# A hybrid layer's prompt block: a third slot for split weights, a new order on VectorE and ScalarE, and taps carried over

## What is computed

```python
h = rmsnorm(x) * (1 + sc1) + sh1
proj = h @ w_in                       # 1024 x 2592
q, k, v, r, zf, zb, ga, gg = split(proj)
gf = log_sigmoid(zf @ w_decay_f + b_decay_f) / TAU        # gb alike
o = gla(q, k, v, gf) + flip(gla(flip(q), ..., flip(gb)))  # chunks of 64 tokens
o = rmsnorm(o) * silu(r)
u = ga * sigmoid(gg)                                      # the GLU product
u = silu(layernorm(depthwise_conv(u, width=31)))          # the taps
x = x + gt1 * (concat(o, u) @ w_out)
# second half: 16 experts, each takes the tokens that score highest for it
x = x + gt2 * expert_choice_moe(rmsnorm(x) * (1 + sc2) + sh2)
```

## Time and profile before

| | before |
|---|---|
| median of 3 runs | 2449.94 us (2448.81 to 2450.29) |
| profiled execution | 2448.1 us, span from first to last instruction 2446.4 us |
| TensorE busy | 2254.9 us, 92% of the span |
| VectorE busy | 1652.5 us, 68% |
| ScalarE busy | 1187.4 us, 49% |
| chain that ended last | 58% of the span on TensorE, 5% on VectorE, 2% on DMA, 2% on ScalarE |
| mean granted TensorE clock | 0.958 |
| median time to landing of the ten stores of split tiles | 13.2 us |
| TensorE busy from 60 to 180 us | 91.9 of 120 us |
| TensorE busy from 180 to 300 us | 119.8 of 120 us |
| VectorE busy from 60 to 180 us | 99.0 of 120 us |

### The profile page before, as it was taken

One profiled execution on the slowest core, in us unless ns is written; L12 is line 12 of the kernel. 1 busy time (PEld: TensorE's weight loads), 2 busy tenths in 40 slices (PEclk: granted clock), 3 DMA queues, 4 the chain that ended last, 5 costly groups with the idle time before them and its releaser, 6 DMA issues.

```text
span 2446.4 us, 43724 instructions
## 1 busy us (share of the span) xinstructions
PE 2254.9 (92%) x16667; PEld 2061.4 (84%) x16667; DVE 1652.5 (68%) x2871; ACT 1187.4 (49%) x1933; POOL 731.4 (30%) x666
## 2 busy tenths in 40 slices
PE   3879999999996999965999999999999999999994
PEld 3768878788885677742999999999999999999994
DVE  1797979799788766448566656666556665566575
ACT  3747364553524444421655554555545555455652
POOL 1000000000001311100254454544545445554352
PEclk8889999999997999986999999999999999999997
DMA  6976666757747566353466677666776667766785
GB/s 227 381 272 219 215 237 233 262 190 261 226 133 260 172 195 203 97 171 112 159 201 187 190 198 208 197 187 188 199 211 194 189 185 203 211 190 190 259 267 193
DMA packets 281300, 505.90 MB, mean 207 GB/s; under 512 B 25793, under 2 KB 224318, under 8 KB 265312
## 3 DMA queue, kind: packets, MB, share of 16 engines
q1 hardware_dynamic: 241872, 377.94, 46.9%
q0 software_dynamic: 39312, 126.38, 19.3%
HBM read 405.74 MB, written 98.53 MB: 206 GB/s over the span
## 4 chain that ended last, share of the span: by engine, by line
PE 58%; DVE 5%; DMA 2%; ACT 2%; issue 1%; POOL 1%; SPq 0%; DVEq 0%; ACTq 0%; POOLq 0%
PE bank L1580 18%; PE bank L1582 18%; PE bank L1581 18%; DVE work_exp L2738 1%; DMA out_dram<-work_exp 1%; PE bank L1833 1%; DVE work_proj L2445 1%; PE bank L1899 1%; PE bank L1843 1%; PE bank L1851 1%; DMA work_exp<-x_rows 1%; ACT hl_exp L1174 0%; DVE work_exp L2984 0%; ACT work_exp L1214 0%; DMA work_exp<-in_b_mod_dram 0%
## 5 line engine op out<-in xcount | busy, mean ns | idle before, releaser
L1580 PE MATMUL bank<-act_hl_exp,hl_exp 128*128 128x288 f32 x3072 | 911.1, 297 | 18.3 <-DVE hl_exp L2901 9.8
L1581 PE MATMUL bank<-act_hl_exp,hl_exp 128*128 128x288 f32 x3072 | 908.2, 296 | 0.0
L1582 PE MATMUL bank<-act_hl_exp,hl_exp 128*128 128x288 f32 x3072 | 906.6, 295 | 0.0
L1580 PEld LDWEIGHTS bank<-act_hl_exp,hl_exp 128*128 128x128 f32 x3072 | 578.4, 188 | 19.8 <-DVE hl_exp L2901 10.7
L1582 PEld LDWEIGHTS bank<-act_hl_exp,hl_exp 128*128 128x128 f32 x3072 | 580.3, 189 | 0.0
L1581 PEld LDWEIGHTS bank<-act_hl_exp,hl_exp 128*128 128x128 f32 x3072 | 579.2, 189 | 0.0
L2901 DVE TENSOR_TENSOR hl_exp<-work_exp,hl_exp 128x1024 fp32r<-128x1024 f32 x192 | 231.3, 1226 | 217.7 <-ACT hl_exp L1174 217.7
L2901 DVE TENSOR_TENSOR hl_exp<-raw_exp,hl_exp 128x1024 fp32r<-128x1024 f32 x192 | 232.1, 1224 | 202.5 <-ACT hl_exp L1174 202.5
L2445 DVE SCALAR_TENSOR_TENSOR work_proj<-work_proj,wcv 128x392 f32<-128x392 f32 (+11 forms) x600 | 337.3, 635 | 0.6
L1174 ACT ACTIVATE hl_exp<-work_exp 128x1024 fp32r<-128x1024 f32 x192 | 199.2, 1055 | 210.4 <-PE bank L1582 205.2
L1174 ACT ACTIVATE hl_exp<-raw_exp 128x1024 fp32r<-128x1024 f32 x192 | 198.6, 1052 | 166.2 <-PE bank L1582 166.2
(11 more groups left out here) (370 smaller groups left out, 3267.4 us busy)
## 6 DMA issues: line engine op xcount, KB each, us to landing
hl_proj<-park_w POOLq DMA_DIRECT2D x80, 1024.0 KB, 6.3
raw_exp<-in_w_e_gate_dram SPq DMA_DIRECT2D x32, 1024.0 KB, 5.9
raw_exp<-in_w_e_up_dram SPq DMA_DIRECT2D x32, 1024.0 KB, 5.9
work_exp<-in_w_e_gate_dram SPq DMA_DIRECT2D x32, 1024.0 KB
work_exp<-in_w_e_up_dram SPq DMA_DIRECT2D x32, 1024.0 KB, 6.5
raw_exp<-in_w_e_down_dram SPq DMA_DIRECT2D x32, 1024.0 KB, 5.8
work_exp<-in_w_e_down_dram SPq DMA_DIRECT2D x32, 1024.0 KB, 6.2
park_w<-hl_proj SPq DMA_DIRECT2D x10, 2048.0 KB, 13.2
```

Of the source, the lines that this page charges most:

```text
L1580: pe.matmul(out, lh, rh, start=first, stop=False)
L1581: pe.matmul(out, lh, rl, start=False, stop=False)
L1582: return pe.matmul(out, ll, rh, start=False, stop=last_)
```

## The change

1. Split tiles get a third slot: `spare_hl`, the columns 256 to 511 of `h_hl`, free during the prompt block. Tiles j = 0 to 9 use slots 0, 1, 2, 0, 1, 2, 0, 1, 0, 1 (`SLOT`), so 2 and 5 are in the third. A split now waits for TensorE and for the store of the tile that had its slot before. The spare slot is stored in four transfers of 512 KB each, whose runs in SBUF are 128 values long. The two raw buffers stay. The first split of the next block's activations, which overwrites the spare slot, waits for its stores.
2. ScalarE's order: the squares of the next block's rows (`x_square`) move from before split 6 to behind `key_ends(b, 0)`; `x_scale` from before value copy 6 to behind value copy 7; `updates(b, 0)` comes before split 9.
3. VectorE's order: low half 7 comes right after the GLU products; the first masks before low half 8; the reciprocal `x_rstd` behind low half 8; second masks right behind low half 9; the second `states` go behind the low parts of the next block.
4. VectorE does taps 0 to 65 in the prompt block and carries 66 to 123 into the first latent block: 14 behind the low part of z, 24 ahead of the first GLU product, 20 between the first and the second. The sigmoids of projection 1 wait only for the first 62 taps of the block before.

```diff
+        spare_hl = h_hl[:, :, :, TP:BT]
...
+        SLOT, SLOT_TURN = (0, 1, 2, 0, 1, 2, 0, 1, 0, 1), (1, 1, 4, 2, 2, 8, 3, 3, 4, 4)
+        SLOT_BEFORE = {j: max(i for i in range(j) if SLOT[i] == SLOT[j]) for j in range(3, NPROJ)}
+
+        def w_part(b, j, q, part_):
+
+            s = SLOT[j] if b.prompt else j % 2
+            return hl[:, s, q, part_] if s < 2 else spare_hl[:, part_, :, 128 * q:128 * q + 128]
...
-                    sp.dma_start(park_w[j], hl[:, j % 2].bitcast(f32)).then_inc(s_wst[j % 2], 16)
+                    if SLOT[j] < 2:
+                        sp.dma_start(park_w[j], hl[:, SLOT[j]].bitcast(f32)).then_inc(s_stored[SLOT[j]], 16)
+                        return
+                    for q in range(2):
+                        for i in range(2):
+                            sp.dma_start(park_w[j, :, q, i], w_part(b, j, q, i).bitcast(f32)).then_inc(s_wst2, 16)
...
-                if j >= 2:
-                    act.wait_ge(s_uh.sem, 2 * (j - 1))
-                    act.wait_ge(s_wst[j % 2], 16 * (j // 2))
+                if j >= 3:
+                    act.wait_ge(s_uh.sem, 2 * (SLOT_BEFORE[j] + 1))
+                    act.wait_ge(s_stored[SLOT[j]], 16 * SLOT_TURN[SLOT_BEFORE[j]])
...
-                x_square(nb, b)
                 proj_hi(b, 6)
                 sigmoid(b, 5, 0)
                 sigmoid(b, 5, 1)
                 proj_hi(b, 7)
-                x_scale(nb)
+                key_ends(b, 0)
+                x_square(nb, b)
                 values(b, 6)
                 proj_hi(b, 8)
-                key_ends(b, 0)
                 values(b, 7)
+                x_scale(nb)
+                updates(b, 0)
                 proj_hi(b, 9)
-                updates(b, 0)
...
                 b.wait(act, s_uh, 2 * NPROJ + 1)
+                act.wait_ge(s_wst2, 16 * SLOT_TURN[5])
...
-                b.wait(act, s_conv, 0)
+                b.wait(act, s_conv, -TAPS // 2 if j == 1 else 0)
...
+                carried(b, 0)
                 if nb is not None and not b.prompt:
                     x_rstd(nb)
                     x_scale(nb)
...
                 proj_lo(b, 2)
+                carried(b, 1)
                 glu(b, 0)
+                carried(b, 2)
                 glu(b, 1)
...
-                taps(b, 12, 20)
+                taps(b, 12, 16)
                 proj_lo(b, 6)
-                x_rstd(nb)
                 glu(b, 2)
                 glu(b, 3)
-                taps(b, 20, 34)
                 proj_lo(b, 7)
-                taps(b, 34, 55)
+                masks(b, 0)
+                taps(b, 16, 30)
                 proj_lo(b, 8)
-                masks(b, 0)
-                taps(b, 55, 72)
+                x_rstd(nb)
+                taps(b, 30, 38)
                 proj_lo(b, 9)
+                masks(b, 1)
                 states(b, 0)
-                taps(b, 72, 83)
-                masks(b, 1)
-                taps(b, 83, 91)
-                states(b, 1)
+                taps(b, 38, 58)
                 modulate_odd(nb, 1)
-                taps(b, 91, 100)
+                taps(b, 58, CARRY[0])
                 lo_rows(nb, 0)
                 modulate_odd(nb, 3)
                 for t in range(1, 4):
                     lo_rows(nb, t)
-                taps(b, 100, TAPS)
+                states(b, 1)
+
+            def carried(b, n):
+
+                if not b.prompt and b.i == 0:
+                    taps(p, CARRY[n], CARRY[n + 1])
+
+            CARRY = (66, 80, 104, TAPS)
```

## The result

The changed kernel takes 2457.81 us (median of 7 runs, 2454.45 to 2461.73), the kernel before beside it 2449.94 us (7 runs, 2447.53 to 2452.81). The ratio is 1.0032, with a 95% interval of 1.0022 to 1.0043: slower by 7.9 us, where +2.0 was forecast. It lies 0.3 us above the range.

The account below looks back on a forecast made before the run. VectorE was taken to set the prompt block's end. Next block 2.5 us sooner, carried taps costing 4.5: +2.0, so 2450.1 on the profiled execution; the median is 1.8 higher, so 2452, range 2443.5 to 2457.5 (8 in 10).

Parts of the forecast that it names:

- VectorE goes through without rest: End of the prompt block: from low half 9, VectorE works 25.0 us without pause, to 164.8 us.
- rival 3: Prompt block: 512 B stores in the full queue take beyond 7.3 us each; at 9.9, sum +7.2, 2457.1; chance 0.16.
- Store 6 and the splits: Prompt block: store 6 lands at 127.6 instead of 123.0, split 8 starts at 127.7, split 9 after 138.6.
- the early splits are won: Prompt block: splits 2 to 7 start earlier with the third slot, but nothing of that gain survives.
- the term of 4.6 us for two stores of 512 B runs: Prompt block: the stores of splits 2 and 5 together delay store 6 by 4.6 us.
- the 2.3 us: Prompt block: extra time of each 512 B store, 2 MiB taking 7.3 instead of 5.0 us; bounds 0 and 4.9.
- Rival 1: Prompt block: packet size costs nothing, everything comes 4.6 us sooner; sum -2.6, 2447.3; chance 0.18.
- The carried taps: First latent block: 58 taps moved there cost 4.5 us, the clock included.
- The second product: First latent block: the second GLU product ends at 39.8 us, TensorE needs it at 36.9 and waits 2.9.
- The 1.5 us of clock: First latent block: lower granted TensorE clock behind the hole costs 1.5 us; bounds 0 and 2.
- Nothing further is late: After that hole: VectorE runs 4.0 us behind its old place, TensorE 4.5, so no further delay.

Follow-up runs that it names:

- four_gates: The changed kernel, but the prompt block's four output-gate tiles go to four separate places; ratio to the kernel before 0.9976 (0.9964 to 0.9989).
- stores_512: The kernel before, with two slots, but the stores of splits 2 and 5 cut into 512 B runs; ratio 1.0001 (0.9991 to 1.0011).
- four_gates_two_slots: The changed kernel with four places for the gate tiles but without the third slot; ratio to the kernel before 0.9988 (0.9977 to 0.9998).
- after_again: The changed kernel, unedited, measured once more on another chip; ratio to the kernel before 1.0005 (0.9992 to 1.0018).
- two_slots: The changed kernel without the third slot, gates' wait and new orders kept; ratio to the kernel before 1.0011 (0.9999 to 1.0023).
- late_loads: The changed kernel, but GpSimd's loads for the first latent block wait until gates 0 and 1 are stored; ratio to before 0.998 (0.9967 to 0.9994).
- before_four_gates: The kernel before, with only the prompt block's four gate tiles given places of their own; ratio 0.9988 (0.9976 to 1.0).

## Why the prediction was wrong

The forecast was z to L 112.4 us (114.9 less 2.5) and L to N 149.9 (145.4 and 4.5). Measured in the profile of after: 118.2 and 147.8.

**VectorE goes through without rest: the step that failed.** Low half 9 to the latent block took 34.8 us (134.93 to 169.76) instead of 25.0. The 25.0 itself was right, as four_gates shows with 24.6. What it left out is ScalarE: from low half 9 on the path was followed on one engine, and not asked when the high parts are ready that VectorE's low rows subtract. In the kernel before they were ready in time, although behind a wait of 2.78 us for a small store. The change brings the gates' stores to the moment at which all four loads of GpSimd are free to go, and it brings ScalarE to gate 2 8.6 us sooner, so the wait grows to 15.25 us. That is +9.8 us, and without it the same kernel is faster than before (four_gates, 0.9976).

The profile of before already held a bound that the forecast broke. Its gate 2 is released 102.1 us behind z (154.59), and from gate 2 to L it takes 12.3 us in after (157.48 to 169.76). By an estimate from these two, a store that lands no earlier than before puts L at 114.4, not at 112.4. The other 3.8 us up to 118.2 are the store's later landing, with all four of GpSimd's loads in flight beside it. None of the rivals held it: rival 3, the slower side, was about the 512 B stores, which cost less than was put down.

**Store 6 and the splits: right in kind, too dear.** Counted from z, split 8 was to start at 75.2, split 9 at 86.1 and low half 9 at 87.3 us. They start at 71.7, 82.3 and 83.4. Splits 8 and 9 do still stand no earlier than before, and the early splits are won, as the step says. But the term of 4.6 us for two stores of 512 B runs measured 3.4 (stores_512), and the slot gave 2.8 back, so about 1 us was left. This is -3.9 us at low half 9, of which 3.5 stand at split 8. (The prediction reads all three waits of the earlier trace rows as waits for a store; at 123.07 the row names none, and ScalarE was idle for 1.01 us only, though store 6 does land at 123.0.) The 284 GB/s behind the 2.3 us came from a short store that was alone; packets of 512 B in the full queue of after go faster (322 GB/s). The packets of 82 to 84 us, and of 99 to 101 (16 KB):

```profile
DMA packets 1272, 0.64 MB, mean 322 GB/s; under 512 B 15, under 2 KB 1272, under 8 KB 1272
...
DMA packets 58, 0.89 MB, mean 443 GB/s; under 512 B 2, under 2 KB 4, under 8 KB 4
```

At 322 instead of the 423 of the earlier trace rows, 2 MiB take 6.5 instead of 5.0 us, 1.5 more, near the 1.7 of stores_512. Rival 1, by which the size costs nothing, is wrong by the same rows. The Trainium skill ("DMA: Bandwidth & Descriptors", the opening table) has 512 B as the smallest transfer at line rate; the measurement differs, and it decides.

**The carried taps: right, but for the clock, which isn't paid in every execution.** The second product was to end 39.8 us behind L and to cost 2.9 us. TensorE resumed 38.9 us behind L after a hole of 2.57. The 1.5 us of clock come in some executions and not in others with nearly the same hole: after has L to N of +2.5 and four_gates_two_slots +1.8 (a hole of 2.55 us), but after_again, two_slots, four_gates and late_loads have +4.0 to +4.7, against the +4.5 that was put down. The stretch of 38 to 46 us behind L, in after, then in after_again:

```profile
207.76:215.76 8.00, 7.06 (x31) 5.86 (x32) 7.93 (x5) 2.06 (x5) 0.53 (x1) 1.00 0.66 197
```
```profile
208.57:216.57 8.00, 6.47 (x22) 5.22 (x23) 7.97 (x6) 1.36 (x3) 0.04 (x1) 0.79 0.65 197
```

The granted clock is 1.00 in the one and 0.79 in the other, a mix of 2.4 and 1.2 GHz, behind holes of 2.57 and 2.58 us. The same stretch has 1.00 in four_gates_two_slots and 0.79 in two_slots, four_gates and late_loads. "Nothing further is late" held too: TensorE is without work for 3.0 us in all from 180 to 300.

**The sum.** -3.9 (low half 9) + 9.8 (the gate's wait) - 2.1 (L to N: the clock not paid in that execution, and a shorter hole) = +3.8 on the forecast of +2.0, the +5.8 of z to N. Behind N the profiled executions differ by another 8.5 us (2142.1 against 2133.6), but the medians by only 2 more than z to N, so most of that is the one execution's. Its next two latent blocks take 143.2 us each, where those of before take 141.7 with the same holes at their starts; after_again, the same kernel, has 141.7 too. The kernel before_four_gates has one block of 143.2, so such blocks come without the change as well. Where the median's other 2 us lie stays open.

## What to carry to other kernels

When a wait is small because of another engine's timing, moving that engine's work can make it large: for every step that is brought forward, list what becomes free to start with it (here GpSimd's loads), and which small transfer that someone waits for must pass through the same DMA engines. Follow the end of a stage back along every engine that feeds it, not only along the one that was last before. And an early buffer pays only if the order of the busiest engine uses the time that it frees.

## What the runs showed of the hardware

- Stores of 128 KB on SyncE's queue took 18.5 us to land while GpSimd's queue held 1 MiB loads, and 7.8 us when these were held back (late_loads). From 145 to 151 us the two queues moved nearly as many packets (307 and 312), but GpSimd's were of 7.4 KB and SyncE's of 0.5 KB: 93.9 and 12.8% of the engines' time, and 2.26 and 0.16 MB.
- SyncE is held while it issues stores with short runs: four transfers took 15.83 and 12.80 us to issue, and the eight of stores_512 13.88 and 11.28, where the same 2 MiB in one transfer of long runs took 0.58 to 5.60 in the kernel before. The DMA engines were busy all the time in these stretches, so what short runs cost into a queue that isn't full was not measured. The raw load behind them is issued only then:

```profile
67.60 15.83 SPq L556 DMA_DIRECT2D park_w<-act_hl_proj  x4
83.53 1.63 SPq L524 DMA_DIRECT2D raw_proj<-in_w_in_dram  x1
...
96.80 12.80 SPq L556 DMA_DIRECT2D park_w<-act_hl_proj  x4
```

- The prompt block takes the same time on the chips that were compared, the rest doesn't: z to L is 118.2 us in after and 118.1 in after_again on another chip. From N to the end before took 2133.6 us (span 2446.4) and before_four_gates, which is the same kernel from there on, 2154.4 us (span 2466.5) on another chip, both at a mean granted clock of 0.958. What makes the difference was not found.
